# A deeper weight ring, a transposed one-hot pick for four experts, and routing woven into the output projection

## The reference

```python
g_prob = softmax(xt @ router_group); g_gate, g_idx = top_k(g_prob, 1)
e_sel = (xt @ router_expert).reshape(T, 4, 8)[arange(T), g_idx[:, 0]]
e_val, e_idx = top_k(e_sel, 2)
gate = g_gate * softmax(e_val)
...
hb = silu(xb @ w_gate[e]) * (xb @ w_up[e])
y = hb @ w_down[e]
```

## Time and profile before

| | us |
|---|---|
| median of 3 runs | 1748.68 (1746.53 to 1750.14) |
| the profiled execution, its own time | 1747.05 |
| its span | 1745.2 |
| PE busy | 1634.0 (94%), 7420 matmuls |
| DVE, ACT, POOL busy | 526.9, 369.8, 223.2 |
| experts of layer 0, first gate/up product to last down product | 320.7 to 796.3 |
| experts of layer 1, the same | 1240.7 to 1714.3 |

### The profile page before, as it was taken

One profiled execution on the slowest core, in us unless ns is written; L12 is line 12 of the kernel. 1 busy time (PEld: TensorE's weight loads), 2 busy tenths in 40 slices (PEclk: granted clock), 3 DMA queues, 4 the chain that ended last, 5 costly groups with the idle time before them and its releaser, 6 DMA issues. The chain is left out here.

```text
span 1745.2 us, 20175 instructions
## 1 busy us (share of the span) xinstructions
PE 1634.0 (94%) x7420; PEld 782.3 (45%) x7420; DVE 526.9 (30%) x1046; ACT 369.8 (21%) x599; POOL 223.2 (13%) x379
## 2 busy tenths in 40 slices
PE   7999997999999999994999999988899999999992
PEld 3444544444444444432577666645333333333330
DVE  4223534321221222224144444433322222222224
ACT  2032421111111111112344445421111111111111
POOL 2000000000000000000144444320000000000000
PEclk9999999999999999996999999999899999999997
DMA  6311033499999999996111112303399999999994
GB/s 217 99 49 54 25 151 145 181 427 429 428 426 428 427 430 428 428 388 245 49 49 49 49 52 99 140 1 145 151 423 428 428 429 429 428 428 428 428 413 168
DMA packets 53953, 463.23 MB, mean 265 GB/s; under 512 B 12800, under 2 KB 12808, under 8 KB 28304
## 3 DMA queue, kind: packets, MB, share of 16 engines
q1 hardware_dynamic: 46336, 445.26, 61.4%
q10 hardware_dynamic: 2448, 8.91, 1.3%
q0 software_dynamic: 5120, 8.40, 1.3%
HBM read 452.03 MB, written 18.89 MB: 270 GB/s over the span
## 5 line engine op out<-in xcount | busy, mean ns | idle before, releaser
L599 PE MATMUL ps<-sb_xh,sb_scr 128*64 128x512 f32 x1024 | 236.7, 602 | 2.4 <-DVE sb_scr L1509 2.4
L622 PE MATMUL ps<-sb_ring_a,sb_scr 128*64 128x512 f32 x1024 | 226.1, 592 | 0.0
L622 PE MATMUL ps<-sb_ring_b,sb_scr 128*64 128x512 f32 x1024 | 225.9, 592 | 0.0
L1527 DVE TENSOR_TENSOR sb_scr<-sb_scr,ps 64x512 f32<-64x512 f32 x64 | 67.6, 1055 | 394.1 <-ACT sb_scr L930 394.1
L755 PE MATMUL ps<-sb_xT,sb_ring_a 128*128 128x512 f32 x384 | 170.4, 598 | 1.1 <-DVE sb_xT L1251 1.1
L1093 POOL DMA_INDIRECT expert_rows<-sb_scr,sb_si x64 | 57.7, 902 | 875.6 <-DVE sb_scr L1548 875.6
L599 PEld LDWEIGHTS ps<-sb_xh,sb_scr 128*64 128x64 f32 x1024 | 86.2, 139 | 137.9 <-issue 137.9
L622 PEld LDWEIGHTS ps<-sb_ring_a,sb_scr 128*64 128x64 f32 x1024 | 88.5, 137 | 131.3 <-issue 131.3
L622 PEld LDWEIGHTS ps<-sb_ring_b,sb_scr 128*64 128x64 f32 x1024 | 83.3, 137 | 135.2 <-issue 135.2
L930 ACT ACTIVATE sb_scr<-ps 64x512 f32<-64x512 f32 x64 | 37.7, 590 | 401.8 <-PE ps L622 401.8
L636 PE MATMUL ps<-sb_ring_a,sb_scr 128*64 128x512 f32 x512 | 118.4, 604 | 1.1 <-issue 1.1
(11 more groups left out here) (230 smaller groups left out, 1626.0 us busy)
## 6 DMA issues: line engine op xcount, KB each, us to landing
sb_ring_b<-in_w_gate_dram SPq DMA_DIRECT2D x32, 2048.0 KB
sb_ring_b<-in_w_up_dram SPq DMA_DIRECT2D x32, 2048.0 KB, 17.2
sb_ring_b<-in_w_down_dram SPq DMA_DIRECT2D x32, 2048.0 KB, 14.8
sb_ring_a<-in_w_gate_dram SPq DMA_DIRECT2D x32, 2048.0 KB
sb_ring_a<-in_w_up_dram SPq DMA_DIRECT2D x32, 2048.0 KB, 17.3
sb_ring_a<-in_w_down_dram SPq DMA_DIRECT2D x32, 2048.0 KB, 15.0
sb_ring_a<-in_c_w_in_dram SPq DMA_DIRECT2D x8, 2048.0 KB, 7.8
sb_ring_a<-in_ab_w_in_dram SPq DMA_DIRECT2D x5, 2048.0 KB, 11.3
```

Source lines behind the costliest of these rows:

```text
L599: mm = nc.tensor.matmul(ps[BR][64 * z:64 * z + CAP, :], me["sel"][:, j, t * CAP:(t + 1) * CAP], xh[:, t, z * 512:(z + 1) * 512], start=(t ...
L622: mm = nc.tensor.matmul(ps[BG][64 * s:64 * s + CAP, :], me["xgT"][:, j, c * CAP:(c + 1) * CAP], wblock(r, s, NC)[:, c, :], start=(c == 0), ...
L1527: return v.tensor_tensor(me["hrow"][0:CAP, :].rearrange("p (c q) -> p q c", c=FC), by_q(me["silu"][64:128, j, :]), by_q(ps[BG][64:128, :]) ...
```

## The change

**Storage.** The two rings, `xh`, `xT` and the scratch become one ring of nine 2 MB slots and a `work` area that share space with the mixers. An expert takes three slots in the order `(3, 4, 5)`, `(6, 7, 1)`, `(2, 0, 8)`, so three experts' weights fit. In layer 0 seven of the first nine loads are issued after the attention; in layer 1 the first expert's after the combine of layer 0, the second's at the mixer's end. Expert e's gate and up load waits for the gate/up products of e - 3.

**Pick.** The rows are no longer normalized and transposed ahead. `h` itself, 128 columns at a stride of 8 elements, is the stationary operand, and a selection of 4 x 64 slots, scaled by `rstd`, streams: the product is already transposed, so `pick_rows`, the ACT copy and `turn_picked` go. A group of 4 experts takes 8 x 4 products of 256 columns, a quarter of them in each expert of the group before.

**Routing.** The router is scaled by the gain once; raw `h` is transposed and its logits are made tile by tile between the pieces of the second half of the output projection. The logits go unscaled into the choice (a positive scale per row changes no maximum) and are scaled before the softmax. The table of row numbers is made in the second expert and the gate values in the fourth.

**The rest.** All 32 experts are written out on every engine, no loops. In layer 1 PE does 11 products of the output projection while the last head is finished. The next mixer's first weight block is loaded after the gate/up products of expert 29, the second and third after the down products of 31. The load of `final_g` moves behind the wait for the last scatters.

```diff
+EXPERT_SLOTS = ((3, 4, 5), (6, 7, 1), (2, 0, 8))
             def out_proj(l, blocks, y, begun):
...
+                for t in range(NT):
+                    for c in range(begun[1][t], NC):
+                        out_part(l, blocks[1], y, t, 1, c)
+                        if t > 0 and c == 1:
+                            turn_raw(l, t - 1)
+                        if t > 0 and c == 3:
+                            logits(l, t - 1)
+                    if t > 0:
+                        positions(l, t - 1)
+                turn_raw(l, NT - 1)
+                pick_first(l, 0)
+                logits(l, NT - 1)
+                pick_first(l, 1)
+                pick_first(l, 2)
+                positions(l, NT - 1)
...
+            def h_cols(t, c):
+                return h[:, t, :].rearrange("p (q c) -> p c q", c=NC)[:, c, :]
...
+            def pick(l, g, b):
+                job = ("pick", l, g, b)
+                pe.wait_ge(sel_ready, (l * (NE // PICK + 3)) + 3 + g + 1)
+                dst = opens(job)
+                for c in (2 * b, 2 * b + 1):
                     for t in range(NT):
+                        mm = nc.tensor.matmul(dst[:, (c % 2) * 256:(c % 2) * 256 + PICK * CAP], h_cols(t, c),
+                                              me["sel"][:, t, :], start=(t == 0), stop=(t == NT - 1))
+                fills(mm, job)
...
+            def expert(l, e):
...
+                fills(mm, ("gu", l, e))
+                if e == 1:
+                    slot_table(l)
+                if e < NE - PICK:
+                    pick(l, g + 1, q)
+                wait_drained(pe, ("gu", l, e))
+                opens(("ht", l, e))
                 pe.sem_inc(turning, 1)
+                fills(turn_hidden(l), ("ht", l, e))
+                s, k = e_in[l * NE + e][2]
+                pe.wait_ge(ring_in[s], 16 * k)
+                wait_drained(pe, ("ht", l, e))
+                opens(("dn", l, e))
+                fills(down(l, three), ("dn", l, e))
...
+            pe.wait_ge(y_ready, HEADS_C - 1)
+            for t in range(NT):
+                out_part(1, w1_in[8], m1["y"], t, 0, HEADS_C - 2)
+            for c in range(HEADS_C - 1):
+                out_part(1, w1_in[9], m1["y"], 0, 1, c)
             pe.wait_ge(y_ready, HEADS_C)
+            out_proj(1, w1_in[8:10], m1["y"], ([HEADS_C - 1] * NT, [HEADS_C - 1, 0, 0, 0]))
...
+            wait_full(sp, ("gu", 0, NE - 3))
+            for i, (s, _) in enumerate(w1_in):
                 if i == 1:
-                    sp.wait_ge(yrow_in[NT - 1], 32)
-                if i == 2:
-                    sp.wait_ge(filled[BY], moe_base[0][BY] + NE)
+                    wait_full(sp, ("dn", 0, NE - 1))
...
+            def select(l, t, e, dst):
+                return v.tensor_scalar(dst, iota[:], slot_key[:, t, e:e + 1], rstd[:, 2 * l + 1, t:t + 1],
+                                       ALU.is_equal, ALU.mult)
...
             def mixer_end(l):
+                add_out(l, 1, 0)
+                for t in range(NT):
+                    copy_raw(l, t)
+                    norm_col(n, t)
+                    choose(l, t)
                     if t < NT - 1:
+                        add_out(l, 1, t + 1)
+                    place_tile(l, t)
```

More of the change, by code:

```diff
@@ L157, in trunk @@
[L157 to L169, removed]
@@ L171, in trunk, with slots @@
-        yrows = flat(ring_b)[:, 0:2 * NT * D].rearrange("p (a d) -> p a d", d=D)
+        def slots(first, count):
+            return ring[:, first:first + count, :].rearrange("p a b -> p (a b)")
+        low, high = work[:, 0:NC * T], work[:, NC * T:]
+        xT = low.rearrange("p (c t) -> p c t", c=NC)
+        xh = ring[:, 8, :].rearrange("p (t d) -> p t d", t=NT)
+        m0 = carve(slots(6, 2), [("q", (4, T)), ("k", (4, T)), ("strip", (2, T)), ("s", (3, T)), ("wa", (4, P)),
+                                 ("wx", (4, P)), ("mx", (32,)), ("nmx", (32,)), ("sum", (32,)), ("rs", (32,))])
@@ L175, in trunk @@
         drained = [sem(f"drained{b}") for b in range(8)]
[L176 removed]
+        ring_in = [sem(f"ring_in{s}") for s in range(SLOTS)]
         x_in = [sem(f"x_in{t}") for t in range(NT)]
@@ new lines, in logits @@
+            def logits(l, t):
+                if t == 0:
+                    pe.wait_ge(router_scaled, 2)
+                for half in range(2):
+                    wait_drained(pe, ("xt", 2 * l + 1, t, half))
+                dst = opens(("lg", l, t))
+                for c in range(NC):
+                    mm = nc.tensor.matmul(dst[:, 0:NG + NE], hx["hT"][:, c, :], rt[:, l, c, :],
+                                          start=(c == 0), stop=(c == NC - 1))
+                fills(mm, ("lg", l, t))
@@ L632, in down, with gate_up @@
-            def down(r):
+            out_proj(0, w0_in[5:7], m0["y"], ([7, 7, 0, 0], [0, 0, 0, 0]))
+            def gate_up(l, slots, j, q, cs=range(NC)):
+                dst = ps[moe_bank(l, 7)]
+                for c in cs:
+                    for z in range(2):
+                        mm = nc.tensor.matmul(dst[64 * z:64 * z + CAP, :], me["xgT"][:, j, c, q * CAP:(q + 1) * CAP],
+                                              wblock(slots[z], NC)[:, c, :], start=(c == 0), stop=(c == NC - 1))
+                return mm
@@ L734, in moe @@
-                expert(l, NE - 2, NE // 2 - 1, 0, ahead=1)
-                expert(l, NE - 1, NE // 2 - 1, 1, ahead=0)
+                pick_first(l, 3)
+                for e in range(NE):
+                    expert(l, e)
                 more_blocks(l)
@@ L850, in norm @@
                         act.wait_ge(x_in[t], 16)
-                    elif n % 2 == 1:
-                        for nb in range(2):
-                            wait_drained(act, ("out", n // 2, t, nb))
                     else:
@@ L1135, in moe @@
+                for e in range(NE):
+                    wait_drained(pool, ("dn", l, e))
+                    scatter_rows(l, e % 2, ri[:, e:e + 1]).then_inc(scattered[e % 2], 16)
                 for j in range(2):
@@ L1556, in more_blocks @@
                     dve.wait_ge(o["pe"], 1)
+                    for j in range(2):
+                        dve.wait_ge(scattered[j], 16 * (l + 1) * (NE // 2))
                     tab = me["tab"][0:CAP, :, :]
@@ L1605, in moe @@
             def moe(l):
-                route(l)
-                dve_expert(l, 0, 0, 0)
-                dve_expert(l, 1, 0, 1)
-                with dve.Fori(1, NE // 2 - 2) as i:
-                    dve_expert(l, i * 2, i, 0)
-                    dve_expert(l, i * 2 + 1, i, 1)
-                dve_expert(l, NE - 4, NE // 2 - 2, 0)
-                dve_expert(l, NE - 3, NE // 2 - 2, 1, ahead=2)
-                dve_expert(l, NE - 2, NE // 2 - 1, 0, ahead=1)
-                dve_expert(l, NE - 1, NE // 2 - 1, 1, ahead=0)
+                for b in range(4):
+                    take_pick(l, 0, b)
+                selections(l, 1)
+                for e in range(NE):
+                    dve_expert(l, e)
                 more_blocks(l)
```

819 lines of the change are left out of this document (374 added, 445 removed).

## The result

The changed kernel takes 1780.51 us (median of 4 runs, 1774.43 to 1782.74) beside 1749.31 for the kernel before (4 runs, 1746.53 to 1750.14): the ratio is 1.0176, with an interval from 1.0148 to 1.0204. It is slower by 31 us, where 1733 was forecast. The profiled executions stand at 1779.7 against 1747.05, 32.7 apart.

The account below looks back on a forecast made before the run. PE was taken to bound the kernel, setting the 14.91 us period per expert. Terms -3.5 - 2.2 + 5 - 13.8 - 2.2 + 1.3 = -15.4 us take 1747.05 to 1731.7, the median 1.6 above, so 1733; range 1718 to 1760.

Parts of the forecast that it names:

- Strided weights: PE's loads of h at stride 8: 1.7 times contiguous, 0.19 us, hidden in picks; raw transposes 1.6 us per tile.
- rival A: In all 64 picks, strided weight loads set the pace, eating the gain from 0.235 us a load; chance 0.14.
- Expert body: PE's work per expert: period 14.89 us for 14.91, a layer's experts 471.4 us, -2.2 us in each layer.
- rival C: In the experts, the removed second transposes were a true cost: 60 x 0.6 us, 1697; chance 0.03.
- The last four experts: End of each layer, no pick left to cover silu and the multiplication: 13.35 us per expert.
- Layer 0: From output projection to first expert in layer 0: 32.2 us against 35.7, so -3.5 us.
- Layer 1: From the last head's sum to the first expert in layer 1: 66.6 us against 80.4, so -13.8 us.
- rival D: Routing's DVE chain too long by 1 us a tile, between-layer cost full: 1742; chance 0.73 together with the forecast.
- Between the layers: Layer 0's last scatter lands later behind two 2 MB blocks and reading back waits: +5 us.
- End: Loading final_g ahead of the rows on ACT's queue at the program's end: +1.3 us.
- Ring: Nine weight slots give nothing in themselves, only room for loads at 15.0 us per expert: cost 0.
- Rival B: Written-out expert code stops PE once per instruction page: 35 pages cost 39 us, 1772; chance 0.06.

Follow-up runs that it names:

- the contiguous variant: The changed kernel with its picks reading 128 adjacent columns of h instead of every eighth: 1744.88 us, 0.9983 of the kernel before.
- the idle transposes: The changed kernel with four idle 128-column transposes between the hidden rows' transposes and down in experts 3 to 31: 1778.7 us, 1.0184 of the kernel before.
- the cut pick: The changed kernel with h read at stride 2, each quarter pick split: 6 products before the hidden rows' transposes, 2 after: 1729.05 us, 0.989 of the kernel before.

## Why the prediction was wrong

**Strided weights** is the step that failed. It took 1.7 for the factor, from DVE's strided write, and put "no cost in the picks". The loads came out 0.239 us apart, 2.1 times the 0.114 of contiguous ones, a little over rival A's point of decision, 0.235; against the contiguous variant the stride costs 30 to 36 us of the 47 by which the forecast of 1733 was missed. The Trainium skill (SBUF — State Buffer, the cacheline note in "Door 1: The DMA port swizzle") was the better guide in size: a halved rate, twice 0.114, is 0.23, and the step at two hits per 16 bytes is where the runs have it, with 196 ns at stride 2 and 330 at stride 4. Its remark that four float32 is how far one may stride freely does not hold for these loads: stride 4 pays nearly in full, 0.235 us. I had read the rule, put its price at 10 us and given A 0.14; the nearest row in count of elements was no row of the unit in question, and with a load at half of the time it hides under, a factor of 2 was the edge itself.

The price of A was too low as well. It charged only the excess of the load over 0.22 us: at 0.239, 1024 records cost 19 us. But a pick whose loads hide has its records 0.216 us apart, and the step from a pick's first product to its second costs another 0.13 us: 0.475 us for each of 64 picks is 30, which is what undoing the stride gives in the timelines.

**Expert body** was right in its structure and missed 0.24 us a period: 14.89 was forecast, and 15.13 is what the contiguous pick gives. I had counted the pick's columns alone, and not what PE loses on entering the pick (PEld idle for 0.81 us, gate and up 6.99 us instead of 6.86, the pick 3.65 instead of 3.57); why it does is open. Over 56 picks the 0.24 us are 13, which explains why even the contiguous variant ends at 1745 rather than at 1733. What this step said of the removed transposes, a gain of 0.02 us because they covered DVE's copy, was shown twice over: by the idle transposes and by the cut pick. So rival C is out.

The last four experts, taken at 13.35 us each, cost 4.8 us more in the two layers, by the lower clock of some down products; 2 us of this was known as layer 0's surplus.

**Layer 0** and **Layer 1** were right: -3.3 for -3.5 and -12.4 for -13.8; the first pick at the lower clock costs the latter 1.35 us. The raw turns even cost less, 1.04 us for 8 at a stride of 8, where 1.6 was taken; the first picks cost more, by 0.5 each, so that the sum came out this near in part by luck. The waits were 0.46, 1.07 and 1.38, 2.9 against 2.4 in all, so rival D, DVE's chain, is not seen. The early products were worth 4.5 by the medians.

**Between the layers** was right, +5.7 for +5, and **End** too, +1.9 for +1.3.

**Ring** was right for the change as forecast, and its reason for the change as made is only stronger. It would have been wrong for a faster PE: at 14.71 us a period, the room is worth 29 us.

**Rival B**, the code: the instruction queue moves 13 packets between 380 and 750 us and 60 in all, and PE's waits have no entry that comes by instruction count. Its 39 us are excluded by the 1744.88 us of the contiguous variant, which is as much written out.

## What to carry to other kernels

Before an operand is read at a stride by TensorE's load, ask how many of its elements fall into 16 bytes: in these picks two were free, one about doubled the load (0.239 us for 0.114), and where the load hides under a product of 256 columns (0.216 us) that makes it the pace. Work removed behind a producer that must be waited for anyway gives nothing until something else is put there. A deeper ring is worth what the compute gains over the loads: measure it together with the faster compute, not on its own.

## What was not expected of the hardware

The same stride costs next to nothing where `h` is transposed. The raw turns' loads are recorded at 191 ns at stride 8, 208 at 4, 206 at 2 and 141 at 1, so they do notice a stride, but 8 transposes take 1.04, 1.12, 1.11 and 1.04 us in the same order, and the step between 2 and 4 elements is not there. Why a transpose's load is spared what a product's load pays is open. The changed kernel, then the one at stride 1:

```profile
L536 PEld LDWEIGHTS ps<-sb_ident,sb_h 128*128 128x128 f32 x64 | 8.2, 191 | 4.0 <-issue 4.0
```
```profile
L545 PEld LDWEIGHTS ps<-sb_ident,sb_h 128*128 128x128 f32 x64 | 7.3, 141 | 4.2 <-issue 4.2
```

Loads of 2 MB into the ring move 425 to 428 GB/s in pieces of 16 KB, 415 with gate and up in pieces of 4 KB and 400 in pieces of 2 KB (down stays at 16 KB), scatters and code among them. And one scatter of 64 rows takes 2.6 us on idle queues and 8.5 behind two 2 MB blocks, although it has a queue of its own.
